# A transformer layer's first projection in three groups of row tiles, with the conditioning product streamed beside the later products

## The reference

```python
ada = (c_act @ w_ada + b_ada)[:, None, :]          # c_act: (1, 2048), w_ada: (2048, 12288)
sh1, sc1, gt1, sh2, sc2, gt2 = jnp.split(ada, 6, axis=-1)
h = _rms(x, g_norm1) * (1 + sc1) + sh1
proj = h @ w_in                                    # (256, 2048) @ (2048, 8256)
... # two attentions: latent (w_uq, w_ukv) and stick-breaking, on parts of proj
merged = jax.nn.sigmoid(gl_a) * (y_a @ w_proj_mla) + jax.nn.sigmoid(gl_b) * (y_b @ w_proj_sb)
x = x + gt1 * (merged @ w_out)
h2 = _rms(x, g_norm2) * (1 + sc2) + sh2
gate, up = jnp.split(h2 @ w_ffn_in, 2, axis=-1)
x = x + gt2 * ((jax.nn.silu(gate) * up) @ w_ffn_out)
```

## Time and profile before

| | us |
|---|---|
| median of 3 runs (2957.64 to 2964.03) | 2961.78 |
| the profiled execution | 2955.05 |
| its span in the trace | 2953.3 |
| PE busy, of the span | 2645.7 (90%) |
| DVE busy | 1698.2 (58%) |
| ACT busy | 1185.8 (40%) |
| read from HBM | 557.69 MB, 190 GB/s over the span |

### The profile page before, as it was taken

The page is one execution under the profiler, slowest core; times in us unless marked ns, Lnnn a source line. Parts: engine busy times, 40 slices in busy tenths (PEclk is TensorE's granted clock), DMA queues, the critical chain, the costliest instruction groups (busy, mean ns, idle before and its releaser), DMA issues.

```text
span 2953.3 us, 35225 instructions
## 1 busy us (share of the span) xinstructions
PE 2645.7 (90%) x12154; PEld 2176.6 (74%) x12154; DVE 1698.2 (58%) x2197; ACT 1185.8 (40%) x1493; POOL 0.2 (0%) x4
## 2 busy tenths in 40 slices
PE   1299999686898999999999899768899999999998
PEld 0277777564676888888888688657788888888886
DVE  6788887766855444545454444565654544545444
ACT  0144443542334444444434444333545444444443
POOL 0000000000000000000000000000000000000000
PEclk9999999898998999999999999979999999999999
DMA  8889997350864666666556666400166666666664
GB/s 302 279 301 321 324 322 251 133 192 3 281 211 137 191 189 187 191 186 190 186 193 192 215 186 192 119 1 1 58 199 187 192 190 187 191 187 185 194 194 159
DMA packets 311134, 561.13 MB, mean 190 GB/s; under 512 B 22968, under 2 KB 76544, under 8 KB 310144
## 3 DMA queue, kind: packets, MB, share of 16 engines
q1 hardware_dynamic: 299696, 545.86, 58.9%
q10 hardware_dynamic: 11344, 14.04, 1.4%
HBM read 557.69 MB, written 2.13 MB: 190 GB/s over the span
## 4 chain that ended last, share of the span: by engine, by line
PE 82%; DVE 10%; DMA 3%; issue 2%; ACT 2%; ACTq 1%; SPq 0%; DVEq 0%
PE ps L448 74%; DVE acc L396 3%; DMA ada_raw<-in_w_ada 3%; DVE w_lo L371 1%; PE ps L1323 1%; PE ps L563 1%; PE ps L480 1%; PE ps L1691 0%; PE ps L1842 0%; PE ps L1871 0%; PE ps L417 0%; DMA raw<-in_w_out 0%; ACT w_hi L340 0%; ACTq L1457 0%; PE ps L276 0%
## 5 line engine op out<-in xcount | busy, mean ns | idle before, releaser
L371 DVE TENSOR_TENSOR w_lo<-raw,w_hi 128x1024 fp32r<-128x1024 f32 x846 | 1035.2, 1224 | 1019.4 <-PE ps L448 982.3
L340 ACT ACTIVATE w_hi<-raw 128x1024 fp32r<-128x1024 f32 x846 | 895.6, 1062 | 1223.0 <-PE ps L448 557.6
L448 PE MATMUL ps<-w_hi,xt_hi 128*128 128x512 f32 x2496 | 983.0, 394 | 30.5 <-DVE w_lo L371 28.9
L448 PE MATMUL ps<-w_hi,xt_lo 128*128 128x512 f32 x2496 | 975.5, 391 | 0.0
L448 PE MATMUL ps<-w_lo,xt_hi 128*128 128x512 f32 x2496 | 975.2, 391 | 0.0
L448 PEld LDWEIGHTS ps<-w_hi,xt_hi 128*128 128x128 f32 x2496 | 471.0, 189 | 141.2 <-issue 36.3
L448 PEld LDWEIGHTS ps<-w_hi,xt_lo 128*128 128x128 f32 x2496 | 470.8, 189 | 99.0
L448 PEld LDWEIGHTS ps<-w_lo,xt_hi 128*128 128x128 f32 x2496 | 471.3, 189 | 95.5
L396 DVE SCALAR_TENSOR_TENSOR acc<-ada_raw,ccol,acc 128x384 f32<-128x384 f32 (+2 forms) x480 | 295.9, 617 | 29.5 <-DMA ada_raw<-in_w_ada 15.3
L448 PE MATMUL ps<-w_hi,ht_hi 128*128 128x512 f32 x704 | 274.7, 390 | 0.0
L448 PE MATMUL ps<-w_hi,ht_lo 128*128 128x512 f32 x704 | 274.1, 389 | 0.0
(11 more groups left out here) (344 smaller groups left out, 1540.6 us busy)
## 6 DMA issues: line engine op xcount, KB each, us to landing
raw<-in_w_in SPq DMA_DIRECT2D x208, 512.0 KB, 4.4
raw<-in_w_ffn_in SPq DMA_DIRECT2D x176, 512.0 KB, 4.4
ada_raw<-in_w_ada SPq DMA_DIRECT2D x96, 512.0 KB, 5.1
ada_raw<-in_w_ada SPq DMA_DIRECT2D x128, 384.0 KB, 4.4
raw<-in_w_ffn_out SPq DMA_DIRECT2D x88, 512.0 KB, 3.7
raw<-in_w_gate SPq DMA_DIRECT2D x88, 512.0 KB, 3.7
raw<-in_w_up SPq DMA_DIRECT2D x88, 512.0 KB, 4.4
raw<-in_w_down SPq DMA_DIRECT2D x88, 512.0 KB, 4.7
```

The costliest lines, as they stand in the source:

```text
L340: act.activation(w_hi[:, w % HI, :, 0:g.width], raw[:, w % RAW, :, 0:g.width], ACT.Copy).then_inc(hi_ready, 1)
L371: dve.tensor_tensor(w_lo[:, w % LO, :, 0:g.width], raw[:, w % RAW, :, 0:g.width], w_hi[:, w % HI, :, 0:g.width].bitcast(F32), ALU.subtract ...
L448: mm = pe.matmul(bank[t][:, 0:g.width], g.lhs(part, 2 * s + k, t), weights[:, k, 0:g.width], start=(s == 0 and k == 0 and n3 == 0), stop=( ...
```

## The change

The ada product becomes one stream (`Ada`): 26 blocks of 512 or 384 columns in the order in which they are needed, each in 8 slots of two row tiles (208 slots). Even and odd row tiles go to two accumulators, `acc` and `acc_odd`, added at a block's end. TensorE sums every block as columns (3 or 4 products with one output column), VectorE adds the bias and keeps the results in `acol`. Only two blocks (16 slots) stand ahead of the products. The first projection is done in three groups of row tiles, `g_in[0]` (tiles 0 to 3, two stations a unit), `g_in[1]` (4 to 9, three) and `g_in[2]` (10 to 15, three), each over all 16 units; ACT copies the first group's sums to `proj`, VectorE adds the other groups' to it. x is turned as it is, by a product with `diag`, which holds 1/rms. Two pairs of tiles are turned at the start and the others at the ends of the groups before theirs (`next_group`). The gates are turned to rows, stored and broadcast without biases. The loops of `g_in`, `g_psb`, `g_uq` and `ffn1.g` are written out. The second norm's shift and scale need no reload.

Where the slots lie is in the list `stations`; SP, VectorE and TensorE hang them on each station by `ada_beside`:

```diff
-ADA = 4
+ADA, ADA_K = 4, 2
-    g_in = Gemm(at, wview("w_in"), KD, 16, lhs_x, ada=(KD // 2, 3 * D // 16))
+    g_in = [Gemm(at, wview("w_in"), n, 16, lhs_x, peeled=8, k0=k0) for k0, n in ((0, 4), (4, 6), (10, 6))]
...
+    class Ada:
+        def load(self, sp, n=1):
+            for v in range(self.loads, self.loads + n):
+                col, width = self.blocks[v // self.per]
+                s = v % self.per
+                if v >= ADA:
+                    sp.wait_ge(ada_used, v - ADA + 1)
+                sp.dma_start(self.tile(v), wview("w_ada")[:, ADA_K * s:ADA_K * (s + 1), col:col + width]
+                             ).then_inc(ada_loaded[v % ADA], 16)
+            self.loads += n
...
+        def multiply(self, dve, n=1):
+            for v in range(self.slots, self.slots + n):
+                b, s = divmod(v, self.per)
+                width = self.blocks[b][1]
+                rows = self.tile(v)
+                dve.wait_ge(ada_loaded[v % ADA], 16 * (v // ADA) + 16)
+                for k, part in enumerate((acc[:, b % 2, 0:width], acc_odd[:, 0:width])):
...
+                    if v >= 1:
+                        dve.wait_ge((ada_even, ada_used)[k], v)
...
+                    ins.then_inc((ada_even, ada_used)[k], 1)
...
     def sync_gemm(sp, g):
         def chunk(u, j, before):
+            for s, w in g.slots(u, j):
+                if j is None:
+                    g.beside.sp(sp, u, s)
+                if (w + (1 - RAW)).above_zero:
+                    sp.wait_ge(raw_used, (w + (1 - RAW)).value)
...
+                sp.dma_start(raw[:, w % RAW, :, :], src).then_inc(loaded[w % RAW], 16)
...
+                    if self.rows:
+                        mm = pe.matmul(o, src, self.rows(t), start=True, stop=True)
+                    else:
+                        mm = pe.transpose(o, src, ident)
...
+    def evac_proj_more(c, u, j):
+        for t in range(T):
+            p = proj[:, t, CW * u:CW * (u + 1)]
+            last = nc.vector.tensor_tensor(p, ps_gemm[2 * (c % 2) + t][:, :], p, ALU.add)
+        last.then_inc(evac_done, 1)
...
+    stations = [(g_in[0], u, s, (2 - s if u < 6 else 1 if u < 13 else 0)) for u in range(16) for s in range(2)]
+    stations += [(g_in[1], u, s, (u < 4 or s < 2) * (u < 14)) for u in range(16) for s in range(3)]
+    stations += [(g_in[2], u, s, 1 if s < 2 else 0) for u in range(16) for s in range(3)]
+    stations += [(None, 0, 0, 8)]
+    stations += [(g_psb, u, s, 1 if s < 3 else 0) for u in range(4) for s in range(4)]
+    stations += [(g_uq, u, s, 1 if u < 2 else 0) for u in range(3) for s in range(2)]
+    stations += [(g_ukv, u, s, 1 if u < 3 else 0) for u in range(4) for s in range(2)]
+    stations += [(None, 0, 1, 10)]
+    stations += [(g_pmla, u, s, 1 if s > 1 else 0) for u in range(4) for s in range(4)]
+    stations += [(g_out, u, s, 1 if s < (6, 5, 5, 0)[u] else 0) for u in range(4) for s in range(8)]
+    stations += [(ffn1.g, u, s, 1 if 1 <= u < 9 and s % 2 == 0 else 0) for u in range(10) for s in range(8)]
...
+    AHEAD = 2
+    def ada_beside(g):
+        sp0, pe0, dve0 = g.beside.sp, g.beside.pe, g.beside.dve
+        def sp(eng, u, s):
+            sp0(eng, u, s)
+            ada.load(eng, min(ada_slots.get((g, u, s), 0), ada.per * len(ada.blocks) - ada.loads))
+        def pe(eng, u, s):
+            pe0(eng, u, s)
+            if (g, u, s) in ada_sums:
+                ada.sum(eng, len(ada_sums[g, u, s]))
+        def dve(eng, u, s):
+            ada.multiply(eng, ada_slots.get((g, u, s), 0))
+            if (g, u, s) in ada_takes:
+                ada.take(eng, len(ada_takes[g, u, s]))
+            dve0(eng, u, s)
...
         def _(sp):
             first_loads(sp)
-            sync_gemm(sp, g_ada)
-            sync_gemm(sp, g_in)
-            sync_gemm(sp, g_psb, (lat_scaled, 4))
+            ada.load(sp, 2 * ada.per + AHEAD)
+            for g in g_in:
+                sync_gemm(sp, g)
+            ada.load(sp, ada_slots[None, 0, 0])
+            sync_gemm(sp, g_psb)
...
-            sync_gemm(sp, g_pmla, (ya_lo, 4))
+            ada.load(sp, ada_slots[None, 0, 1])
+            sync_gemm(sp, g_pmla)
...
         def _(dve):
             start_vector(dve)
-            vector_gemm(dve, g_ada)()
+            ada.multiply(dve, 12)
             small_vector(dve)
-            ada1_vector(dve)
+            ada.multiply(dve, 4)
+            ada.take(dve, 2)
+            turn_x_vector(dve)
```

More of the change, by code:

```diff
@@ L330, in chunk @@
         def chunk(u, j, before):
-            for n, (kind, s, w) in enumerate(g.slots(u, j)):
-                if n == g.hook_at and before and g.S != 2:
+            for s, w in g.slots(u, j):
+                if s == g.hook_at and before and g.S != 2:
                     hook(u - 1, j)
[L334 to L344, removed]
-                        g.beside.act(act, u, s)
+                if g.turn and not before:
+                    g.turn.high(act, s)
+                act.wait_ge(loaded[w % RAW], (w.times(16, RAW) + 16).value)
+                if (w + (1 - HI)).above_zero:
+                    act.wait_ge(w_used, (w + (1 - HI)).value)
+                act.activation(w_hi[:, w % HI, :, :], raw[:, w % RAW, :, :], ACT.Copy).then_inc(hi_ready, 1)
+                if j is None:
+                    if carried and not before and s == min(3, g.S - 1):
+                        carried()
+                    g.beside.act(act, u, s)
@@ new lines, in chunk @@
+                if g.turn and not before:
+                    if s == 0:
+                        g.turn.scaled(dve, 0)
+                    if s + 1 < g.S:
+                        g.turn.scaled(dve, s + 1)
+                    g.turn.low(dve, s)
+                dve.wait_ge(hi_ready, (w + 1).value)
+                if (w + (1 - LO)).above_zero:
+                    dve.wait_ge(w_used, (w + (1 - LO)).value)
+                dve.tensor_tensor(w_lo[:, w % LO, :, :], raw[:, w % RAW, :, :], w_hi[:, w % HI, :, :].bitcast(F32),
+                                  ALU.subtract).then_inc(raw_used, 1)
@@ L401, in chunk @@
+                if j is None:
+                    if carried and not before and s == min(2, g.S - 1):
+                        carried()
+                    g.beside.dve(dve, u, s)
             if g.S == 2 and before:
@@ L860, in turn_x_tensor, with shift_columns @@
-    def turn_x_tensor(pe):
-        pe.wait_ge(xn_ready, 2)
-        pe.wait_ge(start_cols, 4)
+    shifted = sem("shifted")
+    shifted_n = dict(n=0)
+    def shift_columns(dve, vec, ks, gain):
+        r = ROWS[gain][0]
+        dve.wait_ge(ada_taken, ada.takes)
+        dve.scalar_tensor_tensor(scol[:, 0, ks], acol[:, (vec + 1) * KD + ks.start:(vec + 1) * KD + ks.stop], 1.0,
+                                 cols[:, r + ks.start:r + ks.stop], ALU.add, ALU.mult).then_inc(shifted, 1)
+        shifted_n["n"] += 1
+        dve.wait_ge(shifted, shifted_n["n"])
@@ L1286, in down_act @@
             def down_act(act, u, s):
+                if (u, s) == (0, 2) and gate is not None:
+                    gate_load(act, 1, gate)
                 if (u, s) == (0, 4):
@@ new lines, in program @@
+    stations += [(g_out, u, s, 1 if s < (6, 5, 5, 0)[u] else 0) for u in range(4) for s in range(8)]
+    stations += [(ffn1.g, u, s, 1 if 1 <= u < 9 and s % 2 == 0 else 0) for u in range(10) for s in range(8)]
+    ada_slots, ada_sums, ada_takes = {}, {}, {}
+    total, done = 2 * ada.per, 2
+    for i, (g, u, s, n) in enumerate(stations):
+        total += n
+        ada_slots[g, u, s] = n
+        while total >= ada.per * (done + 1):
+            later = [k[:3] for k in stations[i + 1:] if k[0] or k[2] == 0]
+            ada_sums.setdefault(later[1] if g else later[0], []).append(done)
+            ada_takes.setdefault(later[2] if g else later[1], []).append(done)
+            done += 1
@@ new lines, in program @@
+    assert total == ada.per * len(ada.blocks) and done == len(ada.blocks)
+    AHEAD = 2
[13 more added lines that the diff above has]
+            dve0(eng, u, s)
+        g.beside.sp, g.beside.pe, g.beside.dve = sp, pe, dve
```

508 lines of the change are left out of this document (240 added, 268 removed).

## The result

| | before | after |
|---|---|---|
| median of the runs | 2962.76 (4 runs, 2957.64 to 2964.03) | 3016.99 (4 runs, 3014.3 to 3027.81) |
| the profiled execution | 2955.05 | 3016.52 |
| its span | 2953.3 | 3014.7 |

The ratio is 1.0193, with an interval of 1.0165 to 1.0221: slower by 54 us, where 23 had been forecast from the medians (24.6 from the profiled execution). The time lies in the range. The direction and the mechanism hold; the size doesn't. Between the spans of the two profiled executions the difference is 61.4.

A forecast was written before the change was run, and what follows sets the result against it. TensorE, busy 74% of the chain, sets the floor of product stages, with VectorE bounding some projections. The start's -82.9, first projection's +100 and smaller terms sum to +24.6 on 2955.05: 2980, or 2985 as median; range 2935 to 3030.

The forecast's parts named there:

- first product: At the start, products wait for 16 ada slots, not 64: first product at 54.0 instead of 136.9, -82.9 us, bounds +-3.
- first projection: Stations bound by SP's loop of loads: 472 us against 372.1, +100.
- The closed loop: SP's queue, first projection: raw waits behind ada loads for VectorE's slots one or two stations back; +100 us there.
- The turn: First projection, from one used ada slot to the next: 8.5 us, 9.2 with 512 columns, at most two slots each.
- loads land sooner: Rival, first projection and w_proj_sb to w_out: turn 7.75, -34 and -6 us, total 2945; chance 0.14.
- The loop isn't closed: Rival: SP stays ahead, TensorE or VectorE bounds each stage; -104 us in all, 2858; chance 0.12.
- the clock drops in the gaps: Rival: TensorE at half clock, 5.1 us a station, 26 stations lose 22, later stages some 8; 3015; chance 0.16.
- three slots in four stations, two a turn: 13.8 for four: w_proj_sb: 55.2 us plus start against 52.9 before, +3.
- ten slots, five turns, 46: w_uq and w_ukv: 52 us with four stations without slots, before 46.3; +3 together with the gap removed.
- six, five, five slots in eight stations: 27.6 + 24 + 24: w_out: 104 us with the remaining terms, before 98.7; +5 net.
- the 5 us of weights that run ahead: First projection: 5 us taken off the sum of 477 because weights run ahead again where slots are absent.
- hide in TensorE's gaps: First projection: block sums and turns of x cost nothing extra, as TensorE's gaps in the loop cover them.

The follow-up runs named there:

- e1 to e4: Four edits of the changed kernel: raw load before ada loads, AHEAD 0 for 2, AHEAD 1, raw first with AHEAD 0; 2882.48, 2884.14, 2894.94, 2863.31 us.
- e4_both: Changed kernel with SP issuing raw ahead of the ada loads and AHEAD = 0 instead of 2; 2863.31 us, ratio to before 0.9677.
- e7_later_only: Changed kernel with raw loaded ahead of the ada loads only in stages behind the first projection; 2976.81 us, ratio to before 1.0054.
- e5: Changed kernel with the first group's last evacuation on ACT handed to the second group's fourth slot; 3015.40 us, ratio to before 1.0198.
- e6: Changed kernel with raw loads first, AHEAD = 0 and the first group's last evacuation handed to the second group; 2869.98 us, ratio to before 0.9695.
- the control: Changed kernel with raw first, AHEAD = 0 and the last evacuation handed on, rerun on the chip of e10_warm_through; 2868.76 us, ratio to before 0.9691.
- e10_warm_through: The control's kernel plus 78 unread transposes ahead of the heads and 10 in the gap behind them; 2859.77 us, ratio to before 0.9657.
- the same kernel with the carry: Changed kernel with raw first, AHEAD = 0 and the first group's last evacuation handed to the second group; two series, 2869.98 and 2868.76 us.
- the one without the carry: Changed kernel with raw first and AHEAD = 0, last evacuation not handed on; two series, 2863.31 and 2874.38 us.
- e1_raw_first: Changed kernel with SP issuing raw ahead of the ada loads at each station, AHEAD still 2; 2882.48 us, ratio to before 0.9743.

## Where the prediction was right, and the step that failed

By its own terms, in us of the span (measured, forecast):

| | measured | forecast |
|---|---|---|
| first product | -86.5 (at 50.4) | -82.9 |
| first projection | +112.9 | +100 |
| stick-breaking and norms | +2.4 | +4 |
| w_proj_sb | +8.3 | +3 |
| w_uq and w_ukv | +14.8 | +3 |
| heads and MLA | -0.1 | +2 |
| w_proj_mla | -9.4 | -13 |
| w_out | +16.7 | +5 |
| start of ffn1 | -0.9 | -1 |
| ffn1 and what follows | +3.2 | +4.5 |
| sum | +61.4 | +24.6 |

**Right.** The start, though 3.6 us earlier than forecast and so just outside its +-3: the last slot was added up at 41.6, not at 44. The closed loop: SP's raw waits for the slot of the station before, ACT waits for raw, VectorE and DMA fall far below what they were, and changing only the order of two issues or one constant takes 122 to 154 us away (shown by e1 to e4). The turn too: 8.2 us where 8.5 had been forecast, landing 4.39 (4.4). By station it is 7.9 for the first 12, since the last of them already runs at the shorter pitch, and 4.1 for the next 14 (4.25 forecast). So *loads land sooner* fell, which wanted a turn below 7.9: the median over raw of w_in is 4.3 and the first turn shown has 4.4. By the Trainium skill, "DMA: Bandwidth & Descriptors", section on the anatomy of one DMA, whose fit is for transfers issued by GpSimd, 512 KB would take 3.2 us. The transfers here are issued by SP, and the lowest median for 512 KB on the page of the changed kernel is 3.6. *The loop isn't closed* fell as well, but as a price it was good: 2858 for an open loop, and e4_both took 2863.

**The clock.** The rival *the clock drops in the gaps* gave 3015, and the time is 3017; still, it isn't what happened in the place that it named. It wanted 5.1 us a station for the 26 stations with one slot. They are the stretches of 57.7 and 49.5 us, so 4.1 a station, below the 4.25 of the forecast, at a granted 0.91 and 0.93. In the first 12 the clock was lower, 0.70, and there too the loop waited and not TensorE: the two first stretches took 152.1 us where the forecast had 161.5. That the time is near 3015 is luck. In the later stages the granted clock was 0.90, 0.87 and 0.94, against 0.94, 0.93 and 0.98 in e7_later_only; what that is worth by itself no run shows.

**The step that failed** is the size of the loop in the stages behind the first projection: "three slots in four stations, two a turn: 13.8 for four", "ten slots, five turns, 46" and "six, five, five slots in eight stations: 27.6 + 24 + 24". They were costed with the turn of the first projection, its landing raised from 4.4 to 4.8 for 512 columns: 9.2 us. In SP's order of the changed kernel in w_proj_sb the same place of each unit of four stations comes 15.0, 15.1 and 15.3 us after the last, where 13.8 had been forecast; the loads go out in bunches of three there, and land late (DMA issues from 599 to 724 us: KB each, median us from issue to landing):

```profile
600.25 0.37 SPq L290 DMA_DIRECT2D ada_raw<-in_w_ada  x1
600.66 0.98 SPq L356 DMA_DIRECT2D raw<-in_w_proj_sb  x2
...
615.61 0.98 SPq L356 DMA_DIRECT2D raw<-in_w_proj_sb  x2
...
630.67 0.98 SPq L356 DMA_DIRECT2D raw<-in_w_proj_sb  x2
...
645.94 1.17 SPq L356 DMA_DIRECT2D raw<-in_w_proj_sb  x2
```

```profile
raw<-in_w_proj_sb SPq DMA_DIRECT2D x14, 512.0 KB, 5.7
raw<-in_w_ukv SPq DMA_DIRECT2D x8, 512.0 KB, 6.5
raw<-in_w_uq SPq DMA_DIRECT2D x6, 512.0 KB, 6.0
```

A turn with a landing of 5.7 to 6.5 is 0.9 to 1.7 longer, and five of them in w_uq and w_ukv would be 4.5 to 8.5 of the 11.8 missed there. This is an estimate from medians and wasn't tested. The landings alone are not the cost: in e7_later_only the medians in w_proj_sb, w_uq and w_ukv are 6.5, 6.5 and 5.7, and these stages are short, for there the landing isn't in a loop. Another part is an edge that the forecast, a sum of turns, has no term for: between w_uq and w_ukv ACT stands 4.87 us for the last sums before it copies the next weights, and TensorE then 2.69. The kernel before (4.35 and 3.47) and e7_later_only (4.94 and 2.68) have it too. How the 11.8 divide stays open. Over these three stages the miss is 28.8 us (5.3 + 11.8 + 11.7). That it goes with the order of the queue is shown: e7_later_only gives back all of it and 10 more. w_proj_mla also missed, by 3.6 (less gained than forecast). It isn't this loop: the stage took 53.4 us here and 54.6 in e7_later_only.

**The second term that was mis-sized** is the first projection's, by 13. 7.5 lie in the six stations at the end of the first group, 3.7 of them ACT's stand at the last evacuation (shown by e5 and e6), which the forecast didn't have at all: the call that evacuates there also makes ACT wait. The other 3.8, and 4 at the next group's end, are the turns and a block's sum, which "hide in TensorE's gaps": there are no gaps in stations without slots, as its own 16.3 for six stations says. 5.6 are in the 30 stations of 1,1,0, at 9.1 us a group against 8.5. The last 48 stations took 1.5 more, and the 5 us of weights that run ahead weren't there. Against these stand 9.4 us won in the first 26 stations and 1.5 in the 12 after the first group. Of all of it 7 us weren't there in e7_later_only, which has the same code in this stage.

## What to carry to other kernels

In a queue that works in order, a load placed ahead of another passes its wait on: before two streams share a queue, write down for each issue which engine's progress it waits for, and put the stream that the bottleneck needs first and the one with slack behind; here two lines changed the sign of the whole edit, from +54 to -76 us. Work is only hidden by gaps that exist at that very station: cost each addition against the stations where it lies, not against the stage. And where a closed loop contains a transfer, take its landing time from a place where as many transfers are issued together, not from the median of another stage; what such a landing costs depends on whether it is in a loop.

## What the runs showed that was not expected

TensorE can be granted the half clock in the middle of steady work. In the control the clock had come up by the first products of MLA (0.70 at 626.12), and MLA, in which TensorE is busy 19.66 of 20 us, was then granted 0.57 on the mean of 20 us; in e10_warm_through it had 1.00 in the same work. What came ahead of it was a stand of 24.6 us and one of 1.1 us. With the first filled to a rest of 2.82 us, and the second filled, it was absent in all five runs, one by its trace and four by their times (9 us of 2869); with the first filled to a rest of 4.97, in one run of five, by its time. Without any filling the same kernel with the carry never took the shorter time in ten runs, and the one without the carry took it in three of nine. The kernel before, the changed one, e1_raw_first and e5_carried have the same stand of 24.6 us and were granted the full clock in MLA in their profiled executions. So the stand by itself doesn't bring the half clock. That filling it keeps the half clock away is likely, but rests on one series; what decides otherwise stays open. Whether the 78 transposes alone would do, without the 10, wasn't tried.
